# The order of turns and scores in the attention steps with at most four turned blocks

## The reference: what is computed

```
s_c = q . kc * scale + bias ; o_c = softmax(s_c) . vc      # compressed keys, one per 32 tokens
s_s = q . ks * scale + bias ; o_s = softmax(s_s) . vs      # selected blocks: here all causal ones
s_w = q . kw * scale + bias ; o_w = softmax(s_w) . vw      # a window of 512 tokens
out = gate0 * o_c + gate1 * o_s + gate2 * o_w
```

## Time and profile before

| | |
|---|---|
| Median of three runs | 1309.26 us |
| Profiled execution | 1312.92 us, of which the span from first to last instruction 1311.1 us |
| TensorE matmuls | 1178.2 us, 90% of the span |
| TensorE weight loads | 870.7 us, 66% (beside matmuls) |
| VectorE | 713.4 us, 54% |
| ScalarE | 541.1 us, 41% |
| GpSimd | 124.4 us, 9% |
| DMA | 239.78 MB, mean 183 GB/s |
| Mean granted TensorE clock | 0.952 |
| Attention block in the trace | first scores at 384.75 us; the next block's first matmul at 667.76 us |

### The profile page before, as it was taken

One profiled execution on the slowest core, in us unless ns is written; L12 is line 12 of the kernel. 1 busy time (PEld: TensorE's weight loads), 2 busy tenths in 40 slices (PEclk: granted clock), 3 DMA queues, 4 the chain that ended last, 5 costly groups with the idle time before them and its releaser, 6 DMA issues. The chain is left out here.

```text
span 1311.1 us, 21437 instructions
## 1 busy us (share of the span) xinstructions
PE 1178.2 (90%) x7914; PEld 870.7 (66%) x7915; DVE 713.4 (54%) x1415; ACT 541.1 (41%) x936; POOL 124.4 (9%) x180
## 2 busy tenths in 40 slices
PE   3899999999879999999989982799999999999844
PEld 1467667666765666667657862677888887888721
DVE  0212222222346566767667767887565588585256
ACT  0111100010146676666553224665464467464145
POOL 1001021000010000000000001111010012010052
PEclk9799999999989999999999995899999999999977
DMA  9954444320138930000043326999667789693678
GB/s 319 344 170 155 153 180 85 61 85 13 45 101 303 249 76 1 1 2 1 2 131 129 129 96 249 357 373 377 249 225 292 256 289 385 257 357 152 232 264 168
DMA packets 91123, 239.78 MB, mean 183 GB/s; under 512 B 7594, under 2 KB 15461, under 8 KB 90887
## 3 DMA queue, kind: packets, MB, share of 16 engines
q1 hardware_dynamic: 76983, 192.20, 43.3%
q0 software_dynamic: 9296, 31.82, 7.8%
q10 hardware_dynamic: 4768, 14.75, 2.9%
HBM read 200.70 MB, written 44.33 MB: 187 GB/s over the span
## 5 line engine op out<-in xcount | busy, mean ns | idle before, releaser
L2300 PE MATMUL psum<-w_hi,x_parts 128*128 128x512 f32 x736 | 239.1, 396 | 10.3 <-DVE x_parts L2424 8.6
L2417 DVE TENSOR_TENSOR w_lo<-raw,w_hi 128x2048 fp32r<-128x2048 f32 x95 | 213.3, 2288 | 54.0 <-ACT w_hi L2359 53.5
L2359 ACT CAST w_hi<-raw 128x2048 fp32r<-128x2048 f32 x90 | 167.9, 1918 | 61.5 <-DVE work L2435 50.7
L624 PE MATMUL psum<-low,high 128*128 128x512 f32 (+5 forms) x640 | 189.2, 467 | 1.7 <-ACT high L755 1.7
L2300 PEld LDWEIGHTS psum<-w_hi,x_parts 128*128 128x128 f32 x736 | 139.1, 189 | 41.2 <-issue 12.4
L624 PEld LDWEIGHTS psum<-low,high 128*128 128x128 f32 (+1 forms) x640 | 105.4, 182 | 69.7 <-issue 60.2
L2300 PE MATMUL psum<-w_lo,x_parts 128*128 128x512 f32 x368 | 144.0, 391 | 0.0
L2300 PE MATMUL psum<-w_hi,a_parts 128*128 x368 | 120.4, 398 | 5.1 <-DVE a_parts L2430 5.1
L1525 DVE CUSTOM_DVE_ANT_0 low<-psum,high 128x512 f32<-128x512 f32 (+5 forms) x172 | 92.4, 579 | 44.8 <-PE psum L1242 33.7
L1438 ACT ACTIVATE low<-low,high 128x640 f32<-128x640 f32 (+9 forms) x140 | 99.2, 712 | 9.8 <-DVE high L1525 9.5
L1272 PE MATMUL psum<-keep,low 128*128 128x128 f32 (+1 forms) x556 | 93.2, 288 | 8.5 <-ACT high L1478 4.0
(11 more groups left out here) (355 smaller groups left out, 1410.3 us busy)
## 6 DMA issues: line engine op xcount, KB each, us to landing
raw<-in_moe_w_gate SPq DMA_DIRECT2D x16, 2048.0 KB, 11.0
raw<-in_moe_w_up SPq DMA_DIRECT2D x16, 2048.0 KB
raw<-in_moe_w_down SPq DMA_DIRECT2D x16, 2048.0 KB
high<-in_w_mod SPq DMA_DIRECT2D x12, 2048.0 KB, 13.8
y_d<-work ACTq DMA_DIRECT2D x24, 512.0 KB, 6.8
high<-in_x_prompt SPq DMA_DIRECT2D x16, 512.0 KB, 3.6
y_d<-high SPq DMA_DIRECT2D x1, 8192.0 KB, 24.0
low<-in_w_in SPq DMA_DIRECT2D x3, 2048.0 KB, 15.4
```

Of the source, the lines that this page charges most:

```text
L624: mm = pe.matmul(c.bank(2 + n % 2)[lo:lo + T, 0:wide], hT[i % 2][:, k, 0:T], c.w_in[:, k, at:at + wide], start=(k == 0), stop=(k == KT - 1))
L2300: mm = pe.matmul(out, left[l][:, k * P:(k + 1) * P], w[:, bass.ds(at - o + k * step, 512)], start=n == 0, stop=n == len(steps) - 1)
L2359: act.copy(c.w_hi[:, at:at + PART // 2], c.raw[:, o:o + PART // 2]).then_inc(hi_done[p], 1)
L2417: dve.tensor_tensor(low, c.raw[:, o:o + PART // 2], c.w_hi[:, at:at + PART // 2].bitcast(F32), ALU.subtract).then_inc(c.lo_done[p], 1)
```

## The change

In TensorE's stream, where step n-2 has one turn group per head, both heads' turns are issued one after the other, then all score pieces of step n. Before, the first score piece (and with two pieces the second, behind the second turn) was issued as turn, scores, turn. Where step n-2 has two turn groups per head, the order stays as it was: both groups of the first head, all scores, both groups of the second head. What follows in the iteration (compressed branch, gates, keys, output, values, scale turn) stays, as do the streams of the other engines and all waits.

```
                 for m in range(n_turn):
                     turn(n - 2, 0, m)
-                if n_piece:
-                    scores(n, 0)
-                if n_piece == 2 and n_turn != 1:
-                    scores(n, 1)
-                for m in range(n_turn):
-                    turn(n - 2, 1, m)
-                if n_piece == 2 and n_turn == 1:
-                    scores(n, 1)
+                if n_turn == 1:
+                    turn(n - 2, 1, 0)
+                for m in range(n_piece):
+                    scores(n, m)
+                if n_turn == 2:
+                    for m in range(2):
+                        turn(n - 2, 1, m)
```

## The result

The changed kernel took 1324.5 us (median of 4 runs, 1320.26 to 1326.43), the kernel before 1312.24 us beside it: ratio 1.0091, 95% interval 1.0064 to 1.0118, or 8 to 15 us slower. I had forecast 6.8 us slower, 1316.1 us, with a range up to 1323. Of the 8.4 us between 1316.1 and 1324.5, 3.0 are the kernel before, which took 1312.24 us beside the changed one and not 1309.26; 5.4 are the change's own. The direction and the bank waits came as forecast; the clock did not.

What follows compares the result with a forecast made beforehand. TensorE was taken to set the pace in the attention block: stalls of 11.6 us less 4.8 us of saved switches gave 6.8 us slower, 1316.1 us on the median of 1309.26, with a range of 1307 to 1323 us.

Steps and rivals of the forecast that it cites:

- bank waits: Second head's turn waits until an earlier user of the two shared PSUM banks is copied out; stalls of 11.6 us together.
- The clock: Rival: stalls beside long runs of turns lower the granted clock; up to +20 us, 1336 us; chance 0.02.
- Which steps: Only n = 2 to 39 of 70, prompt tiles 0 to 3 and the six sample steps, about 384 to 504 us.
- the sum: Attention block: stalls of 11.6 us less 4.8 us saved by switches, net 6.8 us slower.
- scale turns: Second head's turn waits for ScalarE's copy of the scale turn (L1478); stalls of 5.0 us together.
- sample values: Second head's turn waits for VectorE's two reads of the sample values; stalls of 4.4 us together.
- sample output: Second head's turn waits for VectorE's eight copies of the sample output; stall of 1.3 us.
- gates and keys: Tile 0, n = 4 and n = 6 to 8: waits on VectorE's gate operations and key copies; 0.9 us together.
- the switches: One switch of matmul form less per step, 0.14 us each, 4.8 us saved in all.
- a pair of turns merges: Adjacent turns of both heads save the switch between them; eight adjacent turn blocks take about 1.03 us in tile 3.
- the wait at n = 4: Second head's turn waits for the last of VectorE's gate operations, with scores now behind it; 0.5 us.

Runs made afterwards that it cites:

- e11: The kernel before, unaltered, for a second profile; stage (first scores to eighth scale turn) 126.29 us.
- e12: The changed kernel, unaltered, for a third profile; stage (first scores to eighth scale turn) 135.42 us.
- e2: New order only in the 21 one-group steps not behind another user of the turn banks, old order in the other 17; 0.9987 of the kernel before.
- e3: In all 38 one-group steps the order is scores, both turns, values; 0.9993 of the kernel before.
- e9: The changed kernel with the first turn repeated 2 to 5 times at 13 steps from n = 11 to 37; 1.0053 of the kernel before.
- e8: Order chosen by place in one-group steps: scores, turn, turn; turn, turn, scores; or the old order; 0.9954 of the kernel before.
- e1: New order only in the 17 steps whose first turn comes behind another user of the turn banks, old order elsewhere; 1.0081 of the kernel before.
- e5: The changed order in every one-group step except n = 4; 1.0051 of the kernel before.
- e7: Changed order except at n = 4, first turn repeated three times at n = 14 and five times at n = 29; 1.0059 of the kernel before.
- e10: The changed kernel, unaltered, timed on the same chip as e9; 1.0097 of the kernel before.

## Why the prediction was wrong

- **Which steps, which waits: right.** Thirty-eight steps, nothing beyond them; the releasers were those named. Gaps without a fall or a late rise, against the mean of before and e11, agree with the sum in all pieces but one: to the second scale turn +0.4 (forecast +0.1), to the third +1.2 (+1.0), to the fifth +1.06 (+1.0), to the sixth +2.52 (+2.6), to the seventh +1.02 (+0.7), to the eighth +0.21 (+0.3). The gap to the fourth is +0.2, forecast +1.2: its three waits (0.55, 0.76 and 0.75 us in e12) are the 2.05 us of the sum, but the 0.5 to 0.8 us that TensorE had stood idle at L1347 are gone.
- **The net of waits and switches: right, +6.6 us for 6.8.** The changed kernel without falls is 17.39 + 11.28 + 18.08 + 19.22 + 17.50 + 18.03 + 15.60 + 16.00 = 133.1 us against 126.5, the mean of two profiles of before. Two errors cancel in it, and that is luck. All idle time of TensorE in tiles 0 to 3 grew by 9.8 us (from 4.8 in before to 14.6 in e12; 4.1 in e11), not by 11.6: scale turns +4.4 (forecast 5.0), sample values +4.3 (4.4), sample output +0.9 (1.3), gates and keys +0.6 (0.9), waits for turned blocks +0.4, and 0.8 us less at L1347. And the switches gave about 3.4 us (9.8 less the 6.4 by which 133.1 exceeds the 126.7 of before; 3.7 against e11), not 4.8; at least at one kind of step T1 had already been next to transposes (e2). That a pair of turns merges was right: eight blocks in 1.02 us, against the rule of the Trainium skill weighed there (TensorE: Matmul & The Clock Gate, Part 3, "What overlaps and what doesn't").
- **The clock: the step that failed.** I took the 1.4 us wait at 403.60 that left the clock at 1.00 as proof that such waits do no harm, gave the fall a chance of 0.02 with a price for a long one, and left it out of sum and range. One wait that went well says nothing of a dozen in 90 us. In the three profiles of the changed kernel the time at 1.2 GHz cost 2.65, 2.32 and 2.32 us by falls, and the late rise in one another 1.3: stage +8.9 to +10.6 us instead of +6.6. That denser turns alone bring the clock down is not borne out: e3 has the turns as dense, with one fall, and e9 filled the waits with nothing but transposes, without one; a single profile of each doesn't settle it. The rule that would have it so is the Trainium skill's (same page, Part 4, "PE-mode transpose": transposes don't count for the clock).
- **Open.** The timed differences are 11.9 us (8 to 15) and 12.7 us (9 to 17), the stage explains 8.9 to 10.6. Outside the attention block the span varies from 1023.2 to 1033.7 us between profiles with no relation to the change; one to three profiles per kernel can't say whether falls in the timed runs are more frequent, or whether anything else is in the last 1 to 4 us. What starts a fall was not settled: the added waits and the small matmuls of the sample steps stand at the same places, and no run parts them. Nor was it settled whether the wait at n = 4 makes a late rise likelier.

## What to carry to other kernels

Between two uses of a small ring of buffers, put the work that needs neither: a reordering that brings equal instructions together saves a switch (0.14 us here) and loses a cover (0.4 to 1.5 us) wherever another user of the ring stands next. Ask it for each place of the loop and choose the order by place, as e8 does. In a program with one engine at its limit, count new waits by their length, and give time at the lower clock a term of its own in the sum and the range: here it was 2.3 to 4.0 us beside 6.6.

## What the runs showed of the hardware

- The granted clock fell to the 1.2 GHz level for 3.4 to 6.9 us in a stream in which TensorE was busy for 84 to 95% of the stretches shown, its longest single wait being 1.5 us (changed, e1, e5, e7, e10, e12; also e3 and e8). In the changed kernel it fell at the same step (n = 14) in all three profiles and at n = 29 in one.
- The first rise came 13.7 to 20.3 us after the first scores; in the changed kernel at 20.2 us in one profile and at 14.7 in the two others.
- A switch between transposes and other fp32 matmuls costs 0.14 us, between groups of transposes nothing, even across semaphore waits that are already met: pairs of two, three and four blocks took 0.58, 0.81 and 1.02 us, against 0.37, 0.48 and 0.58 for one group alone.
